# Norms at the borders between stages: squares summed as the rows come, roots on 128x4, the first two tiles of the next product by row block, the output in pieces

## The chip, the cores and the metric

One NeuronCore of a Trainium2 chip. The metric is the device time of one execution in microseconds. Five engines matter: PE (TensorE, matmuls), DVE (VectorE), ACT (ScalarE), POOL (GpSimd) and SP (SyncE, which only issues transfers here). Each runs its own list of instructions in order and waits on semaphores.

## What is computed

Two transformer blocks over one sequence of 512 tokens and 1024 channels, all in float32. The first block has sliding-window attention and a gated linear attention, then a product-key expert layer ("peer"); the second has a feed-forward, latent attention with a gated delta rule, and another feed-forward. What matters here is the normalization in front of the products, seven times in all:

```python
def rmsnorm(x, g):
    xf = x.astype(jnp.float32)
    xf = xf * lax.rsqrt(jnp.mean(xf * xf, axis=-1, keepdims=True) + EPS)
    return (xf * g.astype(jnp.float32)).astype(x.dtype)

def modulate(x, g, shift, scale):
    return rmsnorm(x, g) * (1.0 + scale[:, None, :]) + shift[:, None, :]

h = modulate(x, g_ffn1[l], sh1, sc1)
x = x + 0.5 * gt1[:, None, :] * swiglu(h, w1_gate[l], w1_up[l], w1_down[l])
h = modulate(x, g_mix[l], sh2, sc2)
proj = h @ w_in[l]
...
h = modulate(x, g_ffn2[l], sh3, sc3)
x = x + 0.5 * gt3[:, None, :] * swiglu(h, w2_gate[l], w2_up[l], w2_down[l])
return rmsnorm(x, g_final)
```

## The kernel before, in words

X lies in on-chip memory transposed: 128 channels on the partitions, eight row blocks of 512 tokens side by side (`X[:, k, :]`). The program is a list of stages (L2442 to L2479), and each engine runs its part of each stage in that order: ada1, swa, gla, wout1, query, gates, dense, fin, norm1, ffn1, mix2, delta, state, b1, latent, heads, b2, wout2, ffn2, end. `behind(e, tag)` (L129) makes an engine wait until all four engines have ended a stage. `Marks` (L41) is a semaphore with named values: `then_inc(instruction, key)` counts up after an instruction, `wait_ge(engine, key)` waits for it.

**Weights.** SP loads tiles of 512 KB into a ring of four raw slots (`w_load`, L189). Tiles of kind "split" are turned into two parts: `w_hi` (L207) rounds on ACT, `w_lo` (L216) takes the rest on DVE, into two slots, so the high part of tile i waits until PE has ended tile i-2. `pe_three` (L222) multiplies a tile: for each of eight row blocks three matmuls of 512 columns (high x high, high x low, low x high), 24 in all. `pe_plain` (L233) is the plain float32 product; each float32 matmul shows as two records in the trace.

**A norm** (L293 to L341). ACT squares the eight blocks into four buffers, PE multiplies each square with a 128x128 matrix of ones and adds all eight in bank 0, so that every partition has the sum of each token; DVE takes mean plus epsilon (L308), ACT the root (L299), DVE the reciprocal (L310), all over 128x512. `Modulated` (L313) then has DVE multiply each block by its weight (L330, ahead) and by the reciprocal (L336), ACT add the shift and round it to the high part (L322), and DVE take the low part (L339). PE waits for all eight low parts (L957, L1410, L1583) before the first tile. The final norms scale X itself (L1379, L2437).

The norms are: n1 in ada1 (L414 to L450), n2 ahead of query (L954 to L1002), nf in norm1 and f1 at the head of ffn1, one behind the other (L1367 to L1380, L1406), m2 in mix2 (L1580), f2 at the head of ffn2, ne in end (L2425). In each the work begins behind the previous stage.

**Stages around them.** wout1 (L843) and wout2 (L2394) are eight tiles each, with a residual (L354) by DVE behind each; wout1 has three groups of column sums for the second block's conditioning (`Ada2`, L262) between its tiles. A feed-forward (L1384) multiplies 44 tiles (gate and up in turn), writes high and low parts of 22 hidden blocks, and then 24 down tiles, three for each output block. Its loop over tiles on ACT and DVE splits tile t+1 in iteration t, ahead of the work on tile t:

```python
            for t in range(2 * FF):
                w_lo(e, self.all[t + 1])
```

PE waits for the last hidden block (L1417) between up and down. In query, 16 tiles are followed each by four small matmuls (L970), whose scores DVE copies (L1000) and sorts (`top16`). mix2 first multiplies two narrow tiles (8 columns, t_ab), then a chain on ACT and DVE (L1601 to L1644) with small transposes on PE (L1591), then the qkv tiles. `Branch` (L2067) is b1 and b2; behind b2, the sum YG is split block by block (L346, L351) before wout2. At the end SP waits for all engines and stores X in one transfer (L2505 to L2508).

## Time and profile before

| | |
|---|---|
| time, median of 3 runs | 4030.22 us (4027.99 to 4030.34) |
| the profiled execution, its own time | 4036.27 us |
| its span, first to last instruction | 4034.5 us |
| mean granted TensorE clock | 0.902 |
| PE busy | 3478.3 us, 86% |
| DVE busy | 2137.5 us, 53% |
| ACT busy | 1478.1 us, 37% |
| POOL busy | 740.4 us, 18% |

The profile is one execution as the hardware profiler saw it. Times are in microseconds unless marked ns. "L304" is a line of the kernel. In a timeline a row has the start, the duration from the first to the last of the merged instructions, engine, line, operation, output <- inputs with the shape, the count, and in brackets how long the engine was idle before it and who released it. PEclk is the granted TensorE clock as a share of 2.4 GHz: 1.00, or 0.50 for 1.2 GHz.

### The profile page before, as it was taken

The numbers are of one execution on the slowest core, as the hardware profiler recorded it, in microseconds if no ns is written. First come the engines' busy times: TensorE is split into PE (matmuls) and PEld (weight loads), VectorE is DVE, ScalarE is ACT, GpSimd is POOL, SyncE is SP. The second block draws the span as 40 slices with busy tenths as digits, with TensorE's granted clock in tenths as the row PEclk, the third lists the DMA queues.
The fourth block names the chain that finished last, engine by engine and source line by source line (L and its number), as shares of the span: only waits on it lengthen the run. The fifth ranks groups of instructions, "written<-read, shape, count | busy, mean of one in ns | idle before, by whom it ended". The sixth has DMA issues, their size and how long they took to land.

```text
span 4034.5 us, 40391 instructions
## 1 busy us (share of the span) xinstructions
PE 3478.3 (86%) x16091; PEld 2792.1 (69%) x16091; DVE 2137.5 (53%) x3519; ACT 1478.1 (37%) x2397; POOL 740.4 (18%) x597
## 2 busy tenths in 40 slices
PE   5887883669999999999699977787897898788998
PEld 2466473569999999999488856576666754567886
DVE  2445699967666666666555335565323213334332
ACT  1221115965555555555322224343212212223221
POOL 0100105855444444444100000000000000000000
PEclk7886996889999999999799988898888996899999
DMA  4420511367777777777155321110001120222221
GB/s 165 139 96 16 177 48 45 136 236 292 279 278 279 279 277 276 278 277 256 58 188 187 119 82 47 37 42 1 22 21 63 58 63 0 97 70 84 99 93 69
DMA packets 169292, 537.41 MB, mean 133 GB/s; under 512 B 13840, under 2 KB 65424, under 8 KB 150672
## 3 DMA queue, kind: packets, MB, share of 16 engines
q1 hardware_dynamic: 135696, 346.06, 24.3%
q0 software_dynamic: 33408, 188.76, 12.6%
q8 instruction: 128, 2.10, 0.2%
q14 instruction: 60, 0.49, 0.0%
HBM read 505.41 MB, written 29.36 MB: 133 GB/s over the span
## 4 chain that ended last, share of the span: by engine, by line
PE 77%; DVE 17%; ACT 3%; DMA 2%; issue 1%; SPq 0%; DVEq 0%; ACTq 0%
PE ps L228 10%; PE ps L229 10%; PE ps L230 10%; PE ps L237 5%; PE ps L1277 4%; PE ps L1278 4%; PE ps L1263 4%; PE ps L1261 4%; PE ps L1262 4%; PE ps L1276 4%; DVE peerg_OH L1100 2%; PE ps L304 1%; PE ps L168 1%; PE ps L459 1%; PE ps L255 1%
## 5 line engine op out<-in xcount | busy, mean ns | idle before, releaser
L220 DVE TENSOR_TENSOR Wl<-W,Wh 128x1024 fp32r<-128x1024 f32 x363 | 437.4, 1207 | 581.8 <-ACT Wh L214 581.5
L214 ACT ACTIVATE Wh<-W 128x1024 fp32r<-128x1024 f32 x363 | 375.4, 1036 | 308.3 <-PE ps L230 270.0
L1240 POOL TENSOR_TENSOR peer_Y<-peer_Y,peerv_UV 128x1024 f32<-128x1024 f32 x128 | 379.8, 2967 | 533.7 <-ACT peerv_UV L1301 533.7
L1261 PE MATMUL ps<-peer_Hh,Wh 128*128 128x384 f32 x1024 | 344.4, 336 | 8.4 <-DVE Wl L220 8.4
L1263 PE MATMUL ps<-peer_Hh,Wl 128*128 128x384 f32 x1024 | 344.4, 336 | 0.0
L1262 PE MATMUL ps<-peer_Hl,Wh 128*128 128x384 f32 x1024 | 343.7, 336 | 0.0
L228 PE MATMUL ps<-f_Hh,Wh 128*128 128x512 f32 x704 | 276.9, 393 | 34.2 <-DVE Wl L220 34.2
L1278 PE MATMUL ps<-peerv_VH,peerv_HTl 128*128 128x512 f32 x768 | 301.3, 392 | 0.0
L1277 PE MATMUL ps<-peerv_VL,peerv_HTh 128*128 128x512 f32 x768 | 301.0, 392 | 0.0
L1276 PE MATMUL ps<-peerv_VH,peerv_HTh 128*128 128x512 f32 x768 | 298.7, 389 | 0.9 <-DVE peerv_HTl L1333 0.9
L229 PE MATMUL ps<-f_Hl,Wh 128*128 128x512 f32 x704 | 275.8, 392 | 0.0
L230 PE MATMUL ps<-f_Hh,Wl 128*128 128x512 f32 x704 | 275.7, 392 | 0.0
L1330 DVE TENSOR_TENSOR peerv_TG<-peerv_TG,peerv_GR 128x384 f32<-128x384 f32 x128 | 197.3, 1542 | 141.5 <-ACT peerv_TG L1306 141.5
L228 PE MATMUL ps<-mix_Hh,Wh 128*128 128x512 f32 (+1 forms) x472 | 201.8, 427 | 65.0 <-DVE Wl L220 43.2
L1261 PEld LDWEIGHTS ps<-peer_Hh,Wh 128*128 128x128 f32 x1024 | 192.9, 188 | 13.8 <-DVE Wl L220 8.9
L1262 PEld LDWEIGHTS ps<-peer_Hl,Wh 128*128 128x128 f32 x1024 | 192.8, 188 | 4.9
L1165 PE MATMUL ps<-peerg_OH 128*128 128x128 f32 x768 | 128.7, 333 | 78.1 <-DVE peerg_OH L1100 53.7
L229 PE MATMUL ps<-mix_Hl,Wh 128*128 128x512 f32 (+1 forms) x472 | 195.8, 415 | 0.0
L230 PE MATMUL ps<-mix_Hh,Wl 128*128 128x512 f32 (+1 forms) x472 | 194.2, 412 | 0.0
L1263 PEld LDWEIGHTS ps<-peer_Hh,Wl 128*128 128x128 f32 x1024 | 192.7, 188 | 0.0
L1199 DVE TENSOR_TENSOR peerv_VL<-peerv_VR,peerv_VH 128x1024 fp32r<-128x1024 f32 x128 | 156.8, 1225 | 61.9 <-ACT peerv_VH L1195 61.9
L1165 PEld LDWEIGHTS ps<-peerg_OH 128*128 128x128 f32 x768 | 117.3, 239 | 89.9 <-DVE peerg_OH L1100 69.0
(483 smaller groups left out, 6966.0 us busy)
## 6 DMA issues: line engine op xcount, KB each, us to landing
W<-peer_u SPq DMA_DIRECT2D x128, 512.0 KB, 7.2
peerv_VR<-peer_v SPq DMA_DIRECT2D x128, 512.0 KB, 3.4
gates_dram<-peerg_GB SPq DMA_DIRECT2D x12, 2048.0 KB, 6.8
peerv_GR<-gates_dram SPq DMA_DIRECT2D x32, 768.0 KB, 7.9
f_AW<-w_ada POOLq DMA_DIRECT2D x48, 512.0 KB, 4.3
W<-w_gate SPq DMA_DIRECT2D x44, 512.0 KB, 4.0
W<-w_up SPq DMA_DIRECT2D x44, 512.0 KB, 3.2
swa_AW<-w_ada POOLq DMA_DIRECT2D x32, 512.0 KB, 5.0
```

What stands on the lines that cost most here:

```text
L214: A.then_inc(e.activation(w_parts(i)[0], w_raw(i), ACT.Copy), ("w_hi", i))
L220: V.then_inc(e.tensor_tensor(lo, w_raw(i), hi.bitcast(F32), SUB), ("w", i))
L228: e.matmul(o[0:m, :], hi[:, j, :], rhs[0][:, k, :], start=k == 0, stop=False)
L229: e.matmul(o[0:m, :], hi[:, j, :], rhs[1][:, k, :], start=False, stop=False)
L230: ins = e.matmul(o[0:m, :], lo[:, j, :], rhs[0][:, k, :], start=False, stop=k == nk - 1)
L1240: G.then_inc(e.tensor_tensor(Y, Y, UV[:, k % NUV, 1024:2048], ADD), ("y", k))
L1261: e.matmul(o, hi[:, k, :], H2[0][:, k, 0:TD], start=k == 0, stop=False)
L1262: e.matmul(o, hi[:, k, :], H2[1][:, k, 0:TD], start=False, stop=False)
L1263: ins = e.matmul(o, lo[:, k, :], H2[0][:, k, 0:TD], start=False, stop=k == 7)
L1276: e.matmul(o, HTh[:, s, sl], VH[:, s, d], start=n == 0, stop=False)
L1277: e.matmul(o, HTh[:, s, sl], VL[:, s, d], start=False, stop=False)
L1278: ins = e.matmul(o, HTl[:, s, sl], VH[:, s, d], start=False, stop=n == 127)
```

## The change

- `Norm` replaces the three `rstd` functions. The sum of a block is four matmuls of one column: the squares are the weights, a column of ones the moving operand, so that tokens come to lie on the partitions, one bank column for each block. DVE adds the eight columns (128x4), mean, root and reciprocal run on 128x4, DVE spreads the result on a diagonal (128x512), and one matmul with ones broadcasts it. DVE multiplies X by weight and broadcast in one instruction from the bank (`scale_dve`). Squares lie in three buffers.
- n2, m2, f2 and ne: squares and sums are taken in the stage before, a block's sum behind the tile two blocks later; the last two behind the stage's last tile. nf's follow the residuals of fin, f1's follow the scaling of X by nf. The stage norm1 is gone.
- The first two tiles of the next product are split in the stage before, and `pe_two` multiplies both by row block, as low parts come. The loops in query and in the feed-forward then split tile t+2 in iteration t.
- mix2 splits its first qkv tile ahead of the chain; b2 splits the blocks of YG in its loop; the output goes in eight transfers.

```diff
+    class Norm:
+        def __init__(self, tag, bank, ready):
+            self.tag, self.bank, self.ready, self.s = tag, ps(bank), ready, tiny(4)
+
+        def square(self, k):
+            return DG_t[:, 512 * (k % 3):512 * (k % 3) + 512]
+
+        def sq_act(self, e, k):
+            self.ready(e, k)
+            if k >= 3:
+                PE.wait_ge(e, (self.tag, "sq", k - 3))
+            A.then_inc(e.activation(self.square(k), X[:, k, :], ACT.Square), (self.tag, "sq", k))
+
+        def sq_pe(self, e, k):
+            A.wait_ge(e, (self.tag, "sq", k))
+            for tb, sl in enumerate(sl4):
+                ins = e.matmul(self.bank[:, 8 * tb + k:8 * tb + k + 1], self.square(k)[:, sl], ones[:, 0:1],
+                               start=True, stop=True)
+            PE.then_inc(ins, (self.tag, "sq", k))
+
+        def mean_dve(self, e):
+            PE.wait_ge(e, (self.tag, "sq", 7))
+            V.then_inc(e.tensor_reduce(self.s, self.bank[:, 0:32].rearrange("p (b k) -> p b k", b=4), AX.X, ADD))
+            V.wait_ge(e, V.n)
+            V.then_inc(e.tensor_scalar(self.s, self.s, 1.0 / D, EPS, MUL, ADD), (self.tag, "mean"))
+
+        def root_act(self, e):
+            V.wait_ge(e, (self.tag, "mean"))
+            A.then_inc(e.activation(self.s, self.s, ACT.Sqrt), (self.tag, "root"))
+
+        def root_dve(self, e):
+            A.wait_ge(e, (self.tag, "root"))
+            V.then_inc(e.reciprocal(self.s, self.s))
+            V.wait_ge(e, V.n)
+            V.then_inc(e.tensor_tensor(v4(self.square(8)), bc4(ident), self.s.unsqueeze(2).broadcast_to([128, 4, 128]),
+                                       MUL), (self.tag, "diag"))
+
+        def root_pe(self, e):
+            V.wait_ge(e, (self.tag, "diag"))
+            PE.then_inc(e.matmul(self.bank, ones, self.square(8), start=True, stop=True), (self.tag, "rstd"))
+
+        def scale_dve(self, e, k, o, w, *keys):
+
+            PE.wait_ge(e, (self.tag, "rstd"))
+            V.then_inc(e.scalar_tensor_tensor(out=o, in0=X[:, k, :], scalar=w[:, k:k + 1], in1=self.bank, op0=MUL,
+                                              op1=MUL), *keys)
...
+            self.norm.mean_dve(e)
+            self.norm.root_dve(e)
+            behind(e, self.before)
             for k in range(9):
                 if k < 8:
-                    V.wait_ge(e, (self.tag, "rstd"))
-                    x = self.xw[:, k, :]
-                    V.then_inc(e.tensor_tensor(x, x, self.r, MUL), (self.tag, "xr", k))
+                    if k >= 3:
+                        V.wait_ge(e, (self.tag, "lo", k - 3))
+                    self.norm.scale_dve(e, k, self.xr[:, k % 3, :], self.w, (self.tag, "xr", k))
                 if k:
                     A.wait_ge(e, (self.tag, "hi", k - 1))
                     V.then_inc(e.scalar_tensor_tensor(
-                        out=self.lo[:, k - 1, :], in0=self.xw[:, k - 1, :], scalar=self.shift[:, k - 1:k],
+                        out=self.lo[:, k - 1, :], in0=self.xr[:, (k - 1) % 3, :], scalar=self.shift[:, k - 1:k],
                         in1=self.hi[:, k - 1, :].bitcast(F32), op0=ADD, op1=SUB), (self.tag, "lo", k - 1))
...
+        def pe_two(self, e, outs, ts, m, keys):
+
+            w = [[x.rearrange("p (k m) -> p k m", k=8) for x in w_parts(i)] for i in ts]
+            steps = [(t, k) for k in range(6) for t in (0, 1)] + [(t, k) for t in (0, 1) for k in (6, 7)]
+            for i in ts:
+                V.wait_ge(e, ("w", i))
+            for t, k in steps:
+                V.wait_ge(e, (self.tag, "lo", k))
+                o, (hi, lo) = outs[t][0:m, :], w[t]
+                e.matmul(o, hi[:, k, :], self.hi[:, k, :], start=k == 0, stop=False)
+                e.matmul(o, hi[:, k, :], self.lo[:, k, :], start=False, stop=False)
+                ins = e.matmul(o, lo[:, k, :], self.hi[:, k, :], start=False, stop=k == 7)
+                if k == 7:
+                    PE.then_inc(ins, ("w", ts[t]), keys[t])
...
+            if nb >= 2:
+                n2n.sq_pe(e, nb - 2)
         ada2a.pe(e, 2)
+        n2n.sq_pe(e, 6)
+        n2n.sq_pe(e, 7)
...
+            if nb == 7:
+                w_lo(e, t_q[0])
             if nb == 5:
                 ada2a.dve(e, 0)
             for n in range(3 * nb, 3 * nb + 3):
...
+                   "w2")
+
+    def wout1_act(e):
+        for k in range(8):
+            n2n.sq_act(e, k)
+            if k in (5, 6):
+                w_hi(e, t_q[k - 5])
 
...
+        n2.norm.root_pe(e)
+        n2.pe_two(e, [ps(1), ps(2)], t_q[0:2], 128, [("q", 0), ("q", 1)])
+        for nb in range(1, 17):
+            if 2 <= nb < 16:
+                A.wait_ge(e, ("qt", nb - 2))
+                pe_three(e, ps(1 + nb % 2), t_q[nb], 8, 128, H2, 0, 8, ("q", nb))
...
-                w_hi(e, t_q[nb + 1])
+            if nb < 14:
+                w_hi(e, t_q[nb + 2])
             PE.wait_ge(e, ("q", nb))
             if nb >= 2:
                 PE.wait_ge(e, ("sub", nb - 2))
-            A.then_inc(e.activation(QT[:, nb % 2, :], ps(nb % 2), ACT.Copy), ("qt", nb))
...
         for nb in range(17):
-            if nb < 15:
-                w_lo(e, t_q[nb + 1])
+            if nb < 14:
+                w_lo(e, t_q[nb + 2])
...
             A.then_inc(e.activation(YB[:, blk, 0:512], ps(2 + 2 * blk), ACT.Copy), ("yb", blk))
+        for k in range(8):
+            nf.sq_act(e, k)
+        nf.root_act(e)
+        for k in range(8):
+            f1n.sq_act(e, k)
+            if k < 2:
+                w_hi(e, ff1.all[k])
 
     def fin_dve(e):
...
             residual(e, k, mod1[:, 40:48], ps(FIN_BANK[k]), ("x2", k))
+        ff1.scales(e)
+        nf.mean_dve(e)
+        nf.root_dve(e)
+        for k in range(8):
+            nf.scale_dve(e, k, X[:, k, :], vec("final_norm_w"), ("x3", k))
+        for i in ff1.all[0:2]:
+            w_lo(e, i)
...
+                if nb >= 2:
+                    then.sq_pe(e, nb - 2)
+            then.sq_pe(e, 6)
+            then.sq_pe(e, 7)
...
             self.norm.act(e)
-            w_hi(e, self.all[0])
             for t in range(2 * FF):
-                w_hi(e, self.all[t + 1])
+                w_hi(e, self.all[t + 2])
                 nb = t // 2
...
-            for i in self.all[2 * FF + 1:]:
+            for n, i in enumerate((self.all + ahead)[2 * FF + 2:]):
                 w_hi(e, i)
-
-        def dve(self, e):
+                if n % 3 == 1 and n >= 4:
+                    then.sq_act(e, n // 3 - 1)
+            for k in range(7 if ahead else 6, 8):
+                then.sq_act(e, k)
+
+        def dve(self, e, ahead):
             tag = self.tag
-            behind(e, self.before)
-            V.then_inc(e.scalar_tensor_tensor(out=self.wc, in0=mod2[:, self.m0 + 8:self.m0 + 16], scalar=1.0,
-                                              in1=vec(self.g), op0=ADD, op1=MUL), (tag, "wc"))
-            V.then_inc(e.tensor_scalar(self.hg, mod2[:, self.m0 + 16:self.m0 + 24], 0.5, None, MUL))
-            V.wait_ge(e, V.n)
+            V.wait_ge(e, (tag, "hg"))
             self.norm.dve(e)
-            w_lo(e, self.all[0])
             for t in range(2 * FF):
-                w_lo(e, self.all[t + 1])
+                w_lo(e, self.all[t + 2])
...
                 w_lo(e, i)
                 if self.ada:
                     self.ada.mac(e, 2 * FF + n)
                     if n == 9:
                         self.ada.dve(e, 5)
-                if n >= 3 and n % 3 == 0:
-                    self.x(e, n // 3 - 1)
-            self.x(e, 7)
+                if n % 3 == 2:
+                    self.x(e, n // 3)
+            for nb in range(len(rest) // 3, 8):
+                self.x(e, nb)
 
         def x(self, e, nb):
             PE.wait_ge(e, (self.tag, "d", nb))
             residual(e, nb, self.hg, ps(5 + nb % 3), (self.tag, "x", nb))
 
-    ff1 = FeedForward("f1", "w1", "g_ffn1_2", 0, "norm1", (3, 6))
+    ff1 = FeedForward(f1n, "w1", "g_ffn1_2", 0, "fin", (3, 6))
...
     def mix2_sp(e):
+        for i in t_ab + t_qkv[0:1]:
+            w_load(e, i)
         behind(e, "ffn1")
...
     def mix2_pe(e):
-        behind(e, "ffn1")
-        n4.pe(e)
-        V.wait_ge(e, ("m2", "lo", 7))
-        for s in range(2):
-            pe_three(e, ps(1 + s), t_ab[s], 8, 8, H4, 0, 8, ("ab", s))
+        m2n.root_pe(e)
+        n4.pe_two(e, [ps(2), ps(3)], t_ab, 8, [("ab", 0), ("ab", 1)])
...
         n4.act(e)
-        for i in t_ab:
-            w_hi(e, i)
+        w_hi(e, t_qkv[0])
         PE.wait_ge(e, ("ab", 1))
-        A.then_inc(e.activation(bb[0:8, :], ps(2)[0:8, :], ACT.Sigmoid), "bb")
+        A.then_inc(e.activation(bb[0:8, :], ps(3)[0:8, :], ACT.Sigmoid), "bb")
...
         n4.dve(e)
-        for i in t_ab:
-            w_lo(e, i)
+        w_lo(e, t_qkv[0])
         PE.wait_ge(e, ("ab", 0))
-        V.then_inc(e.tensor_copy(ab[0:8, :], ps(1)[0:8, :]), "ab0")
+        V.then_inc(e.tensor_copy(ab[0:8, :], ps(2)[0:8, :]), "ab0")
...
-                    if self.add:
+                    if self.sums:
                         V.then_inc(e.tensor_tensor(g, g, ps(4 + t % 4), MUL), (tag, "out", t))
                         V.wait_ge(e, (tag, "out", t))
                         V.then_inc(e.tensor_tensor(y, y, g, ADD), (tag, "y", nb))
+                        if nb:
+                            self.sum_dve(e, nb - 1)
...
+        for n, i in enumerate(t_wo2 + ff2.all[0:2]):
             w_hi(e, i)
+            if n >= 4:
+                f2n.sq_act(e, n - 4)
+        for k in range(6, 8):
+            f2n.sq_act(e, k)
...
+        ff2.scales(e)
         x_back.wait_ge(e, "x")
-        for nb in range(9):
-            if nb < 8:
-                w_lo(e, t_wo2[nb])
-            if nb:
-                PE.wait_ge(e, ("wout2", nb - 1))
...
+        for n, i in enumerate(t_wo2 + ff2.all[0:2]):
+            w_lo(e, i)
+            if n >= 2:
+                PE.wait_ge(e, ("wout2", n - 2))
+                residual(e, n - 2, mod2[:, 40:48], ps((n - 2) % 4), ("x4", n - 2))
...
         if "query" in on:
+            for i in t_q[:3]:
+                w_load(e, i)
             query_sp(e)
-            for i in t_q:
+            for i in t_q[3:]:
...
-        for m in engines:
-            m.wait_ge(e, m.last)
-        out_done.then_inc(e.dma_start(out.rearrange("(k p) t -> p k t", p=128), X), "out")
+        for k in range(8):
+            if upto == "end":
+                V.wait_ge(e, ("out", k))
+            else:
+                behind(e, upto)
+            out_done.then_inc(e.dma_start(out[k * 128:k * 128 + 128, :], X[:, k, :]), "out")
         out_done.wait_ge(e, "out")
```

## Rows read from the trace of the kernel before

**Rows 1.** Busy times in windows, the five borders (window, its length, engines' busy time and counts, granted clock, DMA share, GB/s).
```profile
455.70:482.70 27.00, 8.81 (x33) 4.58 (x31) 20.01 (x31) 12.80 (x19) 0.00 (x0) 0.78 0.30 117
1937.50:1994.10 56.60, 23.51 (x65) 11.44 (x65) 35.97 (x51) 21.54 (x33) 2.35 (x3) 0.69 0.08 28
2371.30:2395.80 24.50, 7.11 (x17) 2.96 (x16) 18.84 (x30) 13.19 (x21) 0.00 (x0) 0.72 0.15 46
3617.90:3643.70 25.80, 7.11 (x16) 2.97 (x17) 20.04 (x31) 14.51 (x21) 0.00 (x0) 0.76 0.00 0
4007.80:4034.50 26.70, 7.13 (x16) 2.96 (x16) 10.16 (x11) 6.51 (x10) 0.00 (x0) 0.74 0.22 79
```

**Rows 2.** Timeline from wout1 to query, then two windows of its first tiles.
```profile
458.56 7.10 PE L304 MATMUL ps<-peerq_SQ,consts_sb 128*128 128x512 f32 x16 [1.15 <-ACT peerq_SQ L297]
...
470.48 1.29 DVE L336 TENSOR_TENSOR peerq_XW<-peerq_XW,peerq_RS 128x512 f32<-128x512 f32 x2
...
471.96 0.75 DVE L339 SCALAR_TENSOR_TENSOR peer_Hl<-peerq_XW,small,peer_Hh 128x512 fp32r<-128x512 f32 x1 [0.19 <-ACT peer_Hh L322]
...
482.74 0.76 PE L228 MATMUL ps<-peer_Hh,Wh 128*128 128x512 f32 x1 [17.08 <-DVE Wl L220]
...
482.80:487.40 4.60, 4.60 (x11) 3.63 (x12) 0.93 (x1) 0.00 (x0) 0.00 (x0) 0.50 0.70 219
488.00:494.00 6.00, 6.00 (x28) 4.95 (x27) 1.23 (x1) 1.55 (x2) 0.00 (x0) 1.00 0.00 0
```

**Rows 3.** Timeline of TensorE, one-column sums in three stages, and a window.
```profile
40.90 3.57 PE L255 MATMUL ps<-consts_sb,ada_ACC 128*128 128x1 f32 x16 [16.27 <-DVE ada_ACC L251]
...
446.91 1.84 PE L255 MATMUL ps<-consts_sb,adaw_AA 128*128 128x1 f32 x16
448.62 7.11 PE L237 MATMUL ps<-mix_MX,W 128*128 128x512 f32 x16
...
3224.26 6.22 PE L2141 MATMUL ps<-consts_sb,X 128*128 128x1 f32 x48
...
3229.00:3235.00 6.00, 6.00 (x13) 3.42 (x14) 0.35 (x2) 0.04 (x1) 0.00 (x0) 0.50 0.01 3
```

**Rows 4.** Timeline of the delta stage: scalar step, diagonal and broadcast of a norm.
```profile
2701.61 1.02 PE L1684 MATMUL ps<-DG,consts_sb 128*128 128x512 f32 x2
...
2718.51 0.16 DVE L1733 TENSOR_SCALAR small<-ps 128x4 f32<-128x4 f32 x1 [7.33 <-PE ps L1692]
...
2719.16 0.69 DVE L1737 TENSOR_TENSOR DG<-consts_sb,small 128x512 f32<-128x512 f32 x1
```

**Rows 5.** Timeline of the first stage and of fin and norm1, and a window.
```profile
14.96 9.67 PE L304 MATMUL ps<-ada_SQ,consts_sb 128*128 128x512 f32 x16 [14.96 <-ACT ada_SQ L297]
...
30.19 6.84 DVE L251 SCALAR_TENSOR_TENSOR ada_ACC<-W,small,ada_ACC 128x1024 f32<-128x1024 f32 x5
...
1942.72 0.27 PE L168 MATMUL ps<-consts_sb,peer_Y 128*128 128x128 f32 x1
...
1945.00:1946.00 1.00, 0.00 (x0) 0.00 (x0) 0.33 (x1) 0.58 (x2) 0.00 (x0) 0.62 0.00 0
...
1961.10 5.39 DVE L1379 SCALAR_TENSOR_TENSOR X<-X,vecs_sb,norm_RS 128x512 f32<-128x512 f32 x8
```

**Rows 6.** TensorE's waits in ffn1 (in total, times, longest), and its timeline there.
```profile
PE ps L228 <- DVE f_HFl L1472: 2.2, 1, 2.2
...
2246.98 1.04 ACT L214 ACTIVATE Wh<-W 128x1024 fp32r<-128x1024 f32 x1
...
2248.05 1.23 DVE L220 TENSOR_TENSOR Wl<-W,Wh 128x1024 fp32r<-128x1024 f32 x1 [0.26 <-ACT Wh L214]
```

**Rows 7.** Timeline of TensorE at the end of mix2.
```profile
2423.27 0.76 PE L228 MATMUL ps<-mix_Hh,Wh 128*128 128x512 f32 x1 [3.09 <-DVE Wl L220]
```

**Rows 8.** Timeline of TensorE at the start of wout2.
```profile
3571.70 0.77 PE L228 MATMUL ps<-mlao_Yh,Wh 128*128 128x512 f32 x1 [8.33 <-DVE Wl L220]
```

**Rows 9.** DMA issues by line: size of each, median us to landing.
```profile
W<-w_down SPq DMA_DIRECT2D x16, 384.0 KB, 2.9
```

More of the change, by code:

```diff
@@ L290, in dve @@
             across_dve(e, self.bank, "b_ada_2", self.g0 + i, mod2, (self.tag, "across", i), ("mod2", self.g0 + i))
-    def rstd_act(e, tag, sq, r):
-        for k in range(8):
-            if k >= 4:
-                PE.wait_ge(e, (tag, "sq", k - 4))
-            A.then_inc(e.activation(sq[:, k % 4, :], X[:, k, :], ACT.Square), (tag, "sq", k))
-        V.wait_ge(e, (tag, "mean"))
-        A.then_inc(e.activation(r, r, ACT.Sqrt), (tag, "root"))
-    def rstd_pe(e, tag, sq):
-        for k in range(8):
-            A.wait_ge(e, (tag, "sq", k))
-            PE.then_inc(e.matmul(ps(0), ones, sq[:, k % 4, :], start=k == 0, stop=k == 7), (tag, "sq", k))
@@ L386, in build @@
     PG = Phase("adaw")
[L387 removed]
+    ada2a = Ada2("ada2a", 0, 3, PG, 1, 2)
     PG.end()
@@ L918, in build @@
     P3.end()
-    P3 = Phase("norm")
-    rsf, sqf = P3.t("RS", 512), P3.t("SQ", 2048, k=4)
-    P3.end()
     PP.end()
@@ L1363, in fin_pe, with __init__ @@
             PE.then_inc(ins, ("yt", k))
-    def norm1_act(e):
-        behind(e, "fin")
-        rstd_act(e, "nf", sqf, rsf)
-    def norm1_pe(e):
-        rstd_pe(e, "nf", sqf)
-    def norm1_dve(e):
-        behind(e, "fin")
-        rstd_dve(e, "nf", rsf)
-        V.wait_ge(e, ("nf", "rstd"))
         for k in range(8):
-            V.then_inc(e.scalar_tensor_tensor(out=X[:, k, :], in0=X[:, k, :], scalar=vec("final_norm_w")[:, k:k + 1],
-                                              in1=rsf, op0=MUL, op1=MUL), ("x3", k))
+            nf.sq_pe(e, k)
+        nf.root_pe(e)
+        for k in range(8):
+            f1n.sq_pe(e, k)
     class FeedForward:
-        def __init__(self, tag, n, g, m0, before, ada=None):
-            self.tag, self.g, self.m0, self.before = tag, g, m0, before
+        def __init__(self, norm, n, g, m0, before, ada=None):
+            self.tag = tag = norm.tag
+            self.g, self.m0, self.before = g, m0, before
             P = Phase(tag)
@@ L1473, in dve @@
                                (tag, "hf", nb))
-            rest = self.all[2 * FF + 1:]
+            rest = (self.all + ahead)[2 * FF + 2:]
             for n, i in enumerate(rest):
@@ L2517, in build @@
     for program in (tensor, vector, scalar, gpsimd, sync):
-        for m in engines:
-            m.last = m.n
         program(Tally())
```

194 lines of the change are left out of this document (90 added, 104 removed).

## The prediction

> **What bounds the kernel.** I read the busy times of the stretches between products first. At five borders TensorE is nearly empty: from the last matmul of one product to the first of the next pass 27.0, 56.6, 24.5 and 25.8 us, and 26.7 us from the last one to the end [rows 1], 160.6 us of 4034.5. Elsewhere, in the products, its matmuls stand back to back, so a stretch of it that becomes longer or shorter moves the end. The timeline of the first border shows what fills it: eight full-width sums on PE (7.10 us, to 465.66), mean, root and reciprocal over 512 columns, products and low parts of all eight row blocks (from 470.48), the split of the first weight tile, and only then a matmul at 482.74, 17.08 us after PE's last [rows 2]. Nothing there runs beside anything useful. The borders end one another in turn, so what one gives reaches the end, unless the product behind it meets a later wait.
>
> I count from the profiled execution, 4036.27 us. The median of the runs, 4030.22, is 6.05 lower; the gain is taken over unchanged. About 0.2% (8 us) is what a measurement can tell here.
>
> **Costs common to the borders.** (a) A new sum of a block is four matmuls of one column. Two such sums (16 records) take 1.71 us from their start to the next matmul when PE is hot, so 0.85 each (446.91 to 448.62); in the cold clock 3.57 for two, 1.78 each (at 40.90) [rows 3]. A dense product now holds five of them ahead of its end: +4.25 us; the old eight cost 7.10, but in the gap. (b) From the last sum to the diagonal: a reduce (0.2, like its neighbours) and then what the other norms of this kernel do in 1.34 us (2718.51 to 2719.85); the broadcast matmul takes 1.02 and its weights 0.25 [rows 4]. Together 2.9 with small waits; a cold broadcast adds 0.3. Before, from the last sum to the first product took 4.8 (465.66 to 470.48) [rows 2]. (c) PE starts when block 0 has its low part, 2.2 us after the first product begins (470.48 to 472.71), not after all eight and a weight split [rows 2]. DVE needs 1.3 us per further block; the six matmuls per block of two tiles need 2.6 cold (0.43 each: 11 in 4.6 us) and 1.4 hot (0.23 each: 26 in 6 us, besides two at the window's edges) [rows 2], so DVE keeps ahead, and two tiles last as long as before: some 12 of 48 cold, 13.3 us.
>
> **The clock.** At 3224.26 PE issued 48 one-column records back to back. It was never idle, yet from 3229 the granted clock stands at 0.50, 1.2 GHz, until past 3235, by when full-width matmuls had long followed [rows 3]. So I price sums that follow one another outside a product at the cold value once the clock has fallen. The Trainium skill says otherwise in words (TensorE: Matmul & The Clock Gate, Part 1 and its table of goals): activity releases the throttle, keep TensorE busy and it stays warm. By that rule the sums would get hot by themselves, a rival below; this trace does not agree.
>
> **The edits, border by border.**
> *First norm (n1).* PE is cold there; 8 x 1.78 = 14.2 us from 14.96 give 29.2, then 1.6 to the diagonal and 0.75 for a first multiply: the first multiply-add at 31.6, before at 30.19 [rows 5]. The rest of that stage hangs on DVE and the ring of four weight slots, and moves by **+1.4**. Bounds: -3 (hot after some 5 us, as the old sums there) to +2.
> *Query.* Last tile ends 4.25 later; then a sum, the last ada column sums (1.7) and two sums: 4.25, then 2.9 + 2.2 + 0.35 for one cold sum and latency: first matmul 13.95 after the old end, before 27.0. Gain 13.05. The weight split of tile 2 waits for tile 0, which now ends only six matmuls ahead of tile 1, and DVE splits tile 3 ahead of its first copy of scores: copy 1.5 later after tile 1, but one split (1.1) leaves the DVE chain behind it, which sets that stage: -0.4. **12.6.** SP issues three peer_wq tiles earlier and waits with the subkeys as before; these land long before tile 1 ends.
> *fin, f1.* PE's transposes end at 1943; the sums follow hot for some 2.6 us (the clock fell between 1945 and 1946 before), then cold [rows 5]: 3 x 0.87 + 5 x 1.78 = 11.5, end 1954.7. Cold chain 3.3, so the scaling of X starts at 1958.1, before 1961.10 [rows 5]. The f1 sums run cold, one behind each scaled block: from 1959.5, 14.3 us, to 1973.8; chain 3.3, low part 2.2: first matmul 1979.4, before 1994.1. Gain 14.7. Splits of the first tiles are ready by then.
> *Weight splits two tiles ahead, ffn1 and ffn2.* The third tile waits for its split, which waits for the first tile: 1.05 + 1.23 + latency less the 1.36 of six matmuls = -1.1. And the step from up to down, which looks untouched, gets a new wait. Before, PE waited 2.2 us there for product, high and low part of the last block [rows 6]. Now ACT and DVE do the split of tile all[45] first, and it can start only when PE has ended tile 43: 1.04 + 1.23 us ahead of that chain [rows 6], and in ffn1 a multiply-add (1.37, as each of the five at 30.19) behind it on DVE. -3.7 in ffn1, -2.25 in ffn2. The gap grows to 5.9 and 4.5; more cold matmuls after it: -1.0 and -1.3 (bounds 0 to 2.7 each). f1: 14.7 - 1.1 - 3.7 - 1.0 = **8.9.**
> *m2.* 4.25; two sums, then block 7, whose residual now stands behind the small splits of t_ab (+0.6), square 0.65, sum: last sum at +3.0, chain 2.9, low 2.2, latency 0.2: 12.55 against 24.5, gain 11.95. Abs now waits behind split, copy and add: -1.6. The first qkv tile is split early: the wait of 3.09 after the small transposes goes [rows 7], +3.1. **13.4.**
> *y.* Eight blocks and a tile are split while PE idles 8.33 us, from 3563.4 [rows 8]. Now block 7 only: product, add, high and low part (0.7 each), two small scales (0.35), one tile's low part (1.23, with its high part beside the block's): first matmul 3567.9 instead of 3571.70. **3.8.**
> *f2.* 4.25; the residual of block 7 stands behind split 9, which waits for the last tile: +3.15, square, sum at 4.8, one cold sum 0.3, chain 2.9, low 2.2: 14.55 against 25.8. 11.25 - 1.1 - 2.25 - 1.3 = **6.6.**
> *End.* 4.25; last sum +2.65 (block 7's residual 0.78, square, sum), chain 2.9 with the Sqrt table, eight scalings 5.4 (as 1961.10) [rows 5], one last piece of 256 KB instead of 2 MB: 384 KB land in 2.9 us [rows 9], I take 2.9 for it, and 0.5 of SP and waits. 18.7 against 26.7: **8.0.** Bounds 6 to 9 (queueing behind seven pieces that come every 0.67 us; 2 us for the piece).
> The squares on ACT, the banks and the buffers cost nothing: each square stands between splits that are due later; without that cover a square is 0.65.
>
> Sum: 12.6 + 8.9 + 13.4 + 3.8 + 6.6 + 8.0 - 1.4 = 51.9. 4036.3 - 51.9 = 3984.4; as a median **3978**. Bounds of its own: dense sums 0.78 to 0.95 (20 of them, -2 to +2), clock and gaps +-5, pieces +-2: 3969 to 3989.
>
> **Rivals.**
> A. *The one-column sums run hot.* For: full-width matmuls get hot after some 5 us. Against: 3224 to 3230 [rows 3]. f1: sums of fin end 1950, scaling 1952.9, f1's first matmul 1966.4 instead of 1979.4; first norm 4.7 less: 17.7 more gain, 3961. By the Trainium skill's rule above this is the time. Chance 0.10.
> B. *The pass by row block stays cold* because PE waits in it, four times 48 matmuls at 0.427 = 20.5 instead of 13.3: +28, 4007, still faster. For: at each start the clock is cold. Against: 2.6 us of matmuls per block stand against 1.3 of DVE, so there is no wait. Part of it (one or two borders) lies in 3985 to 3993. Chance 0.08.
> C. *Slower.* The sums inside the products let the clock fall, since such matmuls don't keep it up. Price: a restart costs 12 matmuls x 0.2 = 2.4 plus a cold sum's 0.9, 3.3 each, 20 times 66: 4044. It decides from 2.6 us each (51.9 / 20), and is slower by over 0.2% from 3.0. Against: sixteen such records at 446.91 in a dense stretch, and the 16 records behind took 7.11 us, 0.44 each, the same as the full-width sums of 7.10 [rows 2, 3]. Chance 0.02.
> D. *The new waits are longer than priced* (another queue wait inside the products): half of the gain, 4004. Chance 0.05.
> Forecast as above: 0.75.
>
> **How the numbers follow.** Likeliest 3978. The range takes the forecast's own and A at its lower end, and the first part of B and D at the upper: 3961 to 3992, leaving out some 0.2. Faster by over 0.2%: forecast, A, B, D, 0.96 (all but a little of D); within it 0.02; slower 0.02.
>
> **What would show it.** In the changed profile: five gaps of about 10 to 14 us with one-column sums in them; clock 0.50 during the f1 sums with PE busy; first matmul of a product some 2 us behind the first product on DVE, before the eighth; the wait for HFl between up and down grown from 2.2 to about 6 in ffn1 and 4.5 in ffn2; no idle 3.09 ahead of the first qkv tile; output issues as eight rows, the last within 0.1 us of the last scaling. Wrong would be: sums at 0.87 throughout (A), a matmul step of 0.43 through all 48 (B), cold clock inside ffn down stages (C), or unpredicted waits on split tiles (D).

## The result, and the profile after

The changed kernel takes 4042.27 us (median of 9 runs, 4041.22 to 4044.57), the kernel before 4030.22 (median of 9, 4021.02 to 4033.75): a ratio of 1.0034, interval 1.0024 to 1.0045. It is slower by 12 us, where 3978 was forecast, 52 faster. The profiled execution of it took 4041.22 us, span 4039.4.

I laid the two traces side by side at the first and last matmul of each product (in us; the last column is what the stretch gained or lost, the one before it what the prediction said).

| stretch | before | after | said | measured |
|---|---|---|---|---|
| first norm, to wout1's first matmul | 396.96 | 396.67 | +1.4 | -0.3 |
| wout1, first to last matmul | 58.8 | 64.9 | +4.25 | +6.2 |
| wout1 to query's first matmul | 27.0 | 10.6 | -17.3 | -16.4 |
| query's first matmul to dense's last | 1454.8 | 1455.3 | +0.4 | +0.5 |
| dense to ffn1's first matmul | 56.6 | 39.6 | -14.7 | -17.0 |
| **ffn1, gate and up tiles** | 251.6 | 290.5 | +1.1 | **+38.9** |
| up to down, ffn1 | 2.2 | 5.8 | +3.7 | +3.7 |
| ffn1, down tiles | 123.4 | 129.2 | +5.25 | +5.7 |
| ffn1 to mix2's first matmul | 24.5 | 9.5 | -16.2 | -15.0 |
| mix2's first matmul to b2's last | 1167.5 | 1164.0 | -1.5 | -3.5 |
| b2 to wout2's first matmul | 8.3 | 4.5 | -3.8 | -3.8 |
| **wout2, first to last matmul** | 46.2 | 67.4 | +4.25 | **+21.2** |
| wout2 to ffn2's first matmul | 25.8 | 12.2 | -15.5 | -13.6 |
| ffn2, gate and up tiles | 241.9 | 243.2 | +1.1 | +1.3 |
| up to down, ffn2 | 2.2 | 4.5 | +2.25 | +2.3 |
| ffn2, down tiles | 120.0 | 127.6 | +5.55 | +7.6 |
| last matmul of ffn2 to the end | 26.7 | 13.9 | -12.25 | -12.8 |

The columns add up to 51.9 us less, as said (52.0 by the rounded rows), and 5.0 more, as measured. The five borders behaved, to within 2.3 us each. What ate the gain lies inside two products that the prediction took to be back to back: 37.8 us in ffn1's gate and up tiles and 17.0 in wout2, 54.8 together.

The five borders of the changed kernel, as busy times in windows (window, its length, busy time and count of PE, its weight loads, DVE, ACT, POOL, then granted clock, DMA share, GB/s). They answer to [rows 1]:

```profile
464.20:472.20 8.00, 3.84 (x18) 2.19 (x18) 4.78 (x11) 1.54 (x3) 0.00 (x0) 0.66 0.62 236
1927.60:1967.20 39.60, 30.50 (x165) 27.24 (x165) 19.82 (x35) 16.24 (x26) 1.67 (x3) 0.63 0.20 66
2392.70:2402.20 9.50, 5.00 (x26) 3.25 (x26) 4.42 (x11) 3.71 (x6) 0.00 (x0) 0.64 0.18 55
3638.20:3650.30 12.10, 6.17 (x26) 4.52 (x27) 5.39 (x10) 5.55 (x8) 0.00 (x0) 0.62 0.13 43
4025.60:4039.40 13.80, 4.08 (x25) 2.73 (x24) 7.31 (x13) 2.12 (x3) 0.00 (x0) 0.67 0.40 152
```

The windows before added up to 160.6 us, these add up to 83.0.

Then PE's waits in the whole changed kernel (in total, times, longest). Of the rows shown, the last is new. In the first, 15.0 us are the wait for the program's first square, which the kernel before has too, and 10.4 are new and lie at wout2:

```profile
PE ps L310 <- ACT DG L305: 27.1, 9, 15.0
...
PE ps L255 <- DVE f_AA L251: 19.3, 5, 3.9
```

L255 are the column sums of the conditioning (`Ada2`), which ffn1 carries along between its tiles. Neither the diff nor my prediction speaks of them as touched. The three engines around the first of them, in timelines of the changed kernel:

```profile
2014.30 0.39 PE L230 MATMUL ps<-f_Hh,Wl 128*128 128x512 f32 x1
2018.54 2.39 PE L255 MATMUL ps<-consts_sb,f_AA 128*128 128x1 f32 x16 [3.85 <-DVE f_AA L251]
2020.79 0.77 PE L228 MATMUL ps<-f_Hh,Wh 128*128 128x512 f32 x1
```

```profile
2014.78 1.06 ACT L214 ACTIVATE Wh<-W 128x1024 fp32r<-128x1024 f32 x1 [3.90 <-PE ps L230]
```

```profile
2015.87 1.23 DVE L220 TENSOR_TENSOR Wl<-W,Wh 128x1024 fp32r<-128x1024 f32 x1 [2.82 <-ACT Wh L214]
2017.20 1.28 DVE L251 SCALAR_TENSOR_TENSOR f_AA<-f_AW,small,f_AA 128x1024 f32<-128x1024 f32 x1
```

PE ends tile 7 at 2014.7 and wants the sums of accumulator 0. The last multiply-add into it stands in DVE's iteration 7, behind the split of tile 9. That split needs a slot that tile 7 holds. So the split starts only when PE has ended tile 7: 1.06 on ACT, 1.23 and 1.28 on DVE, and PE waits 3.85 us for all three. Before, iteration 7 split tile 8, into the slot of tile 6, and its multiply-add was done at 2039.75, 0.7 us before PE came for the sums at 2040.45 (1.05 us before at the other four). The cover was thin. DVE's timeline of the kernel before:

```profile
2036.79 1.23 DVE L220 TENSOR_TENSOR Wl<-W,Wh 128x1024 fp32r<-128x1024 f32 x1 [2.06 <-ACT Wh L214]
2038.47 1.28 DVE L251 SCALAR_TENSOR_TENSOR f_AA<-f_AW,small,f_AA 128x1024 f32<-128x1024 f32 x1 [0.46 <-DVE Wl L220]
```

In the changed kernel the wait comes five times, and each time the clock falls. The windows are the wait, the stretch behind it, and the tiles up to the next wait:

```profile
2014.70:2019.00 4.30, 0.46 (x4) 0.46 (x5) 3.03 (x3) 1.06 (x1) 0.22 (x1) 1.00 0.53 179
2019.90:2026.70 6.80, 6.80 (x20) 5.54 (x20) 0.57 (x1) 0.00 (x0) 0.00 (x0) 0.50 0.22 80
2026.70:2067.00 40.30, 40.30 (x179) 33.30 (x178) 20.90 (x21) 11.26 (x14) 3.70 (x7) 1.00 0.49 170
```

Five waits are 19.25 us. The rest of the 37.8, 18.5 or 3.7 for each wait, is PE at half speed behind them.

In wout2 it is the same shape with ACT in the middle. Its queue in the changed kernel, and PE's sum:

```profile
3590.03 1.06 ACT L214 ACTIVATE Wh<-W 128x1024 fp32r<-128x1024 f32 x1 [4.38 <-PE ps L230]
3591.00 0.61 ACT L305 ACTIVATE DG<-X 128x512 f32<-128x512 f32 x1
```

```profile
3589.55 0.39 PE L230 MATMUL ps<-mlao_Yh,Wl 128*128 128x512 f32 x1
3591.66 1.05 PE L310 MATMUL ps<-consts_sb,DG 128*128 128x1 f32 x8 [1.73 <-ACT DG L305]
3592.58 0.48 PE L228 MATMUL ps<-mlao_Yh,Wh 128*128 128x512 f32 x1
```

ACT takes the square of block n-4 behind the high part of tile n. The high part waits until PE has ended tile n-2, and right behind that tile PE wants the sum of block n-4. The waits from 3565 to 3640 (PE's, in total, times, longest) are six of 1.73, five inside wout2 and one behind it:

```profile
PE ps L310 <- ACT DG L305: 10.4, 6, 1.7
```

Inside wout2 the five waits are 8.7 of the 17.0 us; the rest is again mostly PE at half speed, behind four of the five.

### The profile page after: what moved, and what is told of

It is laid out like the page before. It is cut to its first block, busy times and chain, and to the rows that moved or that the text cites. A ratio compares the mean times of both kernels' runs of the same rounds, so it can differ in the third digit from the quotient of the medians.

```text
span 4039.4 us, 41152 instructions
## 1 busy us (share of the span) xinstructions
PE 3534.0 (87%) x16441; PEld 2863.0 (71%) x16441; DVE 2102.5 (52%) x3501; ACT 1479.5 (37%) x2397; POOL 738.3 (18%) x597
## 4 chain that ended last, share of the span: by engine, by line
PE 78%; DVE 16%; ACT 3%; DMA 2%; issue 1%; SPq 0%; DVEq 0%; ACTq 0%
PE ps L228 10%; PE ps L229 10%; PE ps L230 10%; PE ps L237 5%; PE ps L1327 4%; PE ps L1328 4%; PE ps L1313 4%; PE ps L1311 4%; PE ps L1312 4%; PE ps L1326 4%; DVE peerg_OH L1150 2%; PE ps L310 2%; PE ps L255 1%; PE ps L168 1%; DVE Wl L220 1%; PE ps L507 1%
## 5 line engine op out<-in xcount | busy, mean ns | idle before, releaser
L228 PE MATMUL ps<-f_Hh,Wh 128*128 128x512 f32 x672 | 266.9, 397 | 2.2 <-DVE Wl L220 2.2
L229 PE MATMUL ps<-f_Hl,Wh 128*128 128x512 f32 x672 | 265.4, 395 | 0.0
L230 PE MATMUL ps<-f_Hh,Wl 128*128 128x512 f32 x672 | 265.1, 395 | 0.0
L228 PE MATMUL ps<-mix_Hh,Wh 128*128 128x512 f32 x456 | 194.3, 426 | 45.7 <-DVE Wl L220 23.4
L229 PE MATMUL ps<-mix_Hl,Wh 128*128 128x512 f32 x456 | 188.5, 413 | 0.0
L230 PE MATMUL ps<-mix_Hh,Wl 128*128 128x512 f32 x456 | 187.4, 411 | 0.0
```

What stands on the lines that cost most here:

```text
L228: e.matmul(o[0:m, :], hi[:, j, :], rhs[0][:, k, :], start=k == 0, stop=False)
L229: e.matmul(o[0:m, :], hi[:, j, :], rhs[1][:, k, :], start=False, stop=False)
L230: ins = e.matmul(o[0:m, :], lo[:, j, :], rhs[0][:, k, :], start=False, stop=k == nk - 1)
```

## The experiments

All kernels are compared with the kernel before in the same job, whose medians were 4030.2, 4027.1, 4030.0 and 4032.7; experiments that have the changed kernel as base stand against its 4042.3. **Theory W**: work that waits for PE's tile was put ahead of work that PE waits for behind the same tile; the cost is the wait and the half-speed stretch behind it. **Rival S**: the one-column sums themselves let the clock fall. **Rival M**: weight transfers are late. "Hot" and "cold" stand for a granted clock of 1.00 and 0.50; a one-column record is one of the two that a one-column float32 matmul leaves in the trace, so a block's sum is eight of them.

**e1, the multiply-add ahead of the split** (ffn1, DVE):

```diff
             for t in range(2 * FF):
-                w_lo(e, self.all[t + 2])
                 if self.ada:
-                    if t % 8 == 1 and t > 8:
-                        self.ada.dve(e, t // 8 - 1)
                     self.ada.mac(e, t)
+                w_lo(e, self.all[t + 2])
+                if self.ada and t % 8 == 1 and t > 8:
+                    self.ada.dve(e, t // 8 - 1)
```

> Edit: in ffn1 DVE does the multiply-add of the conditioning of iteration t ahead of the split of tile t+2, not behind it. Theory W (a wait with its price in clock): the five waits of 3.85 us ahead of the column sums vanish, and so do the 13 or so matmuls at half speed behind each (38.9 us that ffn1's gate and up tiles grew by, less 5 x 3.85 = 19.3, is 19.6): 4042 becomes 4003. Rival S (the one-column sums themselves let the clock fall, wait or not): only the 19.3 go, 4023, and the granted clock still falls behind the sums. Rival M (the 38.9 us come from weight transfers that are late): 4042, no change.

Measured: 4003.51 us (4000.64 to 4005.06), ratio to before 0.9937, 0.9920 to 0.9953. Gate and up tiles take 252.8 us instead of 290.5. A window from the third tile to the last, of e1:

```profile
1982.70:2220.60 237.90, 237.90 (x1088) 198.01 (x1088) 131.12 (x132) 68.38 (x85) 22.72 (x43) 1.00 0.58 187
```

PE is never idle in it, and the clock is 1.00 throughout, with all five groups of sixteen one-column records inside. S and M fall for this stage. Moving two lines is worth 38.8 us, and the one edit alone puts the changed kernel ahead of the one before. (The step from up to down also fell by 1.4, to 4.45: the multiply-add of 1.28 no longer stands in that chain, which the expectation had left out.)

**e2, the square ahead of the high part** (wout2, ACT):

```diff
-            w_hi(e, i)
             if n >= 4:
                 f2n.sq_act(e, n - 4)
+            w_hi(e, i)
```

> Edit: in wout2 ACT takes the square of block n-4 ahead of the high part of tile n, not behind it. The high part waits until PE has ended tile n-2, and PE's sum of block n-4 stands right behind that tile. Theory W: the five waits of 1.9 us inside wout2 vanish with the slow matmuls behind them, and wout2 shrinks by 21.2 - 4.25 = 17.0 us: 4025. Rival S: the waits go, 5 x 1.9 = 9.4, and the clock still falls behind the sums: 4033.

Measured: 4024.36 us (4019.80 to 4028.50), ratio 0.9993, 0.9984 to 1.0003. wout2 takes 51.2 us instead of 67.4; what is left of these waits is, in PE's waits of e2 from 3570 to 3634:

```profile
PE ps L310 <- ACT DG L305: 1.6, 2, 0.9
```

The five sums between tiles stand back to back with the matmuls, clock 1.00; the 1.6 us lie behind the last tile. 51.2 is 5.0 above the kernel before, for five sums priced at 4.25.

**e3, both, and the second down tile's split behind the last hidden block:**

```diff
 @@ ACT, in the loop over tiles @@
-                w_hi(e, self.all[t + 2])
+                if t < 2 * FF - 1:
+                    w_hi(e, self.all[t + 2])
 @@ ACT, behind the loop @@
+            w_hi(e, self.all[2 * FF + 1])
 @@ DVE, in the loop over tiles @@
-                w_lo(e, self.all[t + 2])
+                if t < 2 * FF - 1:
+                    w_lo(e, self.all[t + 2])
 @@ DVE, behind the loop @@
+            w_lo(e, self.all[2 * FF + 1])
```

> Edit: both of the above, and ACT and DVE split the second down tile behind the last hidden block instead of ahead of it, in both feed-forwards. Theory W: 38.9 + 17.0, and the step from up to down goes back from 5.8 and 4.45 to 2.2 us each (5.9), with some 1 us of slow matmuls behind: 4042 - 62 = 3980, what the prediction said for the change, plus 2. Rival S: 19.3 + 9.4 + 6: 4007.

Measured: 3978.00 us (3975.51 to 3982.81), ratio 0.9880, 0.9863 to 0.9896. PE's waits of e3 from 1980 to 2349, in ffn1 and behind it:

```profile
PE ps L228 <- DVE f_HFl L1542: 2.2, 1, 2.2
PE ps L310 <- ACT DG L305: 0.3, 1, 0.3
```

The step from up to down is back at 2.2, as in [rows 6], and so is ffn2's. The change with three orders of work put right gives 49 us against the before of its job. No run has the third edit alone; e1 and e2 together give 56.7 of e3's 64.3, which leaves 7.6 for it, where 6.9 was expected.

**e4, the wait without the sums behind it** (ffn1, PE):

```diff
                 if self.ada and t % 8 == 7:
-                    self.ada.pe(e, t // 8)
+                    V.wait_ge(e, (self.ada.tag, "mac", t))
+                if self.ada and t % 8 == 0 and t:
+                    self.ada.pe(e, t // 8 - 1)
```

> Edit: in ffn1 PE still waits for the multiply-adds behind tiles 7, 15, 23, 31, 39, but issues the sixteen one-column records of their sums one tile later, so that full matmuls follow the wait at once. If the wait alone lets the clock fall: 4042 as the changed kernel, clock 0.50 behind each wait. If it takes the wait and the one-column matmuls together: the 19.6 us of slow matmuls go and the waits stay, 4022.

Measured: 4031.84 us (4027.15 to 4034.59), between the two. PE's waits of e4 in ffn1, and windows of one wait, of the slow stretch behind it and of the tiles that follow:

```profile
PE ps L228 <- DVE f_AA L251: 19.3, 5, 3.9
```

```profile
2010.60:2014.60 4.00, 0.15 (x1) 0.00 (x0) 2.56 (x3) 1.06 (x1) 0.00 (x0) 1.00 0.47 160
2016.10:2019.40 3.30, 3.30 (x9) 2.55 (x8) 0.44 (x1) 0.00 (x0) 0.00 (x0) 0.50 0.47 158
2019.50:2061.00 41.50, 41.50 (x192) 34.60 (x191) 20.91 (x21) 11.25 (x14) 3.59 (x7) 1.00 0.49 160
```

The waits are what they were, 3.85 each, and the clock still falls behind every one, but behind this one it is cold for 3.3 us of the window instead of 6.8. Gate and up tiles take 282.3: against e1's 252.8, less the waits, that is 2.0 us of slow matmuls for each wait; with the sums straight behind the wait it was 3.7. So the wait alone lets the clock fall, and sixteen one-column records behind it nearly double what that costs. Neither branch of the expectation was right alone. The Trainium skill (TensorE: Matmul & The Clock Gate, "HAM oscillation — how this bites in real kernels") tells of a kernel whose loop waits for a transfer each time round and pays for a fall of the clock each time; the five waits here agree.

**e5, no row-block pass.** Base of e5 to e8: e3, 3978.0.

```diff
-            for i in ts:
-                V.wait_ge(e, ("w", i))
-            for t, k in steps:
...
+            V.wait_ge(e, (self.tag, "lo", 7))
+            for t in (0, 1):
+                pe_three(e, outs[t], ts[t], 8, m, (self.hi, self.lo), 0, 8, keys[t])
```

> Base: the kernel with the three edits (3978.0). Edit: the first two tiles of query, ffn1, mix2 and ffn2 wait for the low part of all eight blocks and are then multiplied one after the other, as every other tile. From the first to the eighth low part DVE takes 8.8 us at each of the four borders; the wait of 1.1 us ahead of the third tile goes at three of them. By the prediction's reading (PE is never held up within the row-block pass): 4 x 8.8 - 3 x 1.1 = 32 more: 4010. If the row-block pass stayed cold for its length (rival B of the prediction), the two orders would cost the same to within some 5 us: 3978 to 3985.

Measured: 4009.95 us (4006.83 to 4016.59), ratio 0.9949, 0.9933 to 0.9966. PE's waits of e5 ahead of the first tiles of ffn1 and mix2 (in the row-block pass of the changed kernel they are 2.6 and 2.5 us):

```profile
PE ps L228 <- DVE f_Hl L366: 11.4, 1, 11.4
PE ps L228 <- DVE mix_Hl L366: 11.3, 1, 11.3
```

The row-block pass is worth 32 us of the change's gain at the borders. Rival B of the prediction falls; the pass is cold for its first 9 to 12 matmuls, as every product's start, and hot for the rest: from the first to the last of its 48 starts it takes 12.4 to 13.1 us in the changed kernel, said 13.3.

**e6, the output in one transfer:**

```diff
-        for k in range(8):
...
-            out_done.then_inc(e.dma_start(out[k * 128:k * 128 + 128, :], X[:, k, :]), "out")
+        V.wait_ge(e, ("out", 7))
+        out_done.then_inc(e.dma_start(out.rearrange("(k p) t -> p k t", p=128), X), "out")
```

> Base: the kernel with the three edits. Edit: the output leaves in one transfer of 2 MB behind the last scaling. The transfer takes 7.3 us as in the kernel before instead of 2.2 for the last piece: 5 more, 3983. If the pieces queued behind one another, the gain would be smaller and the whole within 2 us: 3980.

Measured: 3976.05 us (two runs, 3974.53 and 3977.57), lower than either number expected, which by itself would say that the pieces bring nothing. The profile says where to look. DMA issues of e3, then of e6 (KB each, us from issue to landing):

```profile
out<-X SPq DMA_DIRECT2D x8, 256.0 KB, 2.2
```

```profile
out<-X SPq DMA_DIRECT2D x1, 2048.0 KB, 7.2
```

From ffn2's last matmul to the end of the span, e3 has 3973.7 - 3959.6 = 14.1 us and e6 19.3 (to 3975.8), so the pieces are worth 5.2 at that place. e6's stream merely came there 3.2 us earlier, through stretches in which the two kernels do not differ. Ahead of wout1 the changed kernel and e1 to e9 do not differ, yet its first matmul lies between 391.9 and 396.8 in them: a difference of a few us between single profiles, or between medians of two runs, is not to be read without its place.

**e7, squares and sums behind the last tile** (mix2's, ffn2's and the last norm; PE's part, ACT's squares are moved alike):

```diff
-                if nb >= 2:
-                    then.sq_pe(e, nb - 2)
-            then.sq_pe(e, 6)
-            then.sq_pe(e, 7)
+            for k in range(8):
+                then.sq_pe(e, k)
```

> Base: the kernel with the three edits. Edit: for the norms of mix2, ffn2 and end, ACT's squares and PE's sums stand behind the last tile of the stage ahead, all eight, not between its tiles (the one-column form stays). Cold theory, as the prediction priced it: three sums at 0.85 and five at 1.78 us = 11.5 from the last tile to the last sum, against 3.5, 5.65 and 2.6 now, and 4.05 less inside each stage: 10.5 more, 3988. Hot rival (one-column sums keep the clock up): 6.8 per border, 3.5 less in all: 3974.

Measured: 3988.36 us (3986.51 to 3990.21), ratio 0.9897, 0.9880 to 0.9913. The sums behind wout2 in e7, and two windows of them:

```profile
3580.34 12.17 PE L310 MATMUL ps<-consts_sb,DG 128*128 128x1 f32 x64 [1.73 <-ACT DG L305]
```

```profile
3578.50:3582.00 3.50, 1.77 (x16) 1.67 (x15) 1.89 (x2) 3.13 (x5) 0.00 (x0) 1.00 0.00 0
3582.30:3592.10 9.80, 9.80 (x47) 9.80 (x48) 0.00 (x0) 3.80 (x5) 0.00 (x0) 0.50 0.11 46
```

64 one-column records, back to back behind a wait of 1.73: the clock falls 1.8 us after their start and stays down while PE is busy for 9.8. The changed kernel's own trace says the same: of the two norms behind dense, the first one's eight sums begin in a hot stretch, and the second one's are cold from end to end (clock 0.50 from 1938 to 1972), 13.81 us where 14.3 was said:

```profile
1932.84 8.99 PE L310 MATMUL ps<-consts_sb,DG 128*128 128x1 f32 x64
1947.07 13.81 PE L310 MATMUL ps<-consts_sb,DG 128*128 128x1 f32 x64 [1.50 <-ACT DG L305]
```

The cold reading of [rows 3] holds; rival A of the prediction falls, and with it, for matmuls of this form, the rule that it drew on (Trainium skill, TensorE: Matmul & The Clock Gate, Part 1). Squares and sums between the tiles of the stage ahead are worth 10 us at three borders.

**e8, a version that goes further**, three more places where PE waits for what it does not yet need:

```diff
 @@ PE, from up to down: wait for the hidden blocks that the tile reads @@
-            V.wait_ge(e, (tag, "hf", FF - 1))
                 for i, k0, n in self.down[nb]:
+                    if nb == 0:
+                        V.wait_ge(e, (tag, "hf", k0 + n - 1))
 @@ row-block pass: four blocks of both tiles, then the rest of each @@
-            steps = [(t, k) for k in range(6) for t in (0, 1)] + [(t, k) for t in (0, 1) for k in (6, 7)]
+            steps = [(t, k) for k in range(4) for t in (0, 1)] + [(t, k) for t in (0, 1) for k in range(4, 8)]
 @@ mix2, PE: the first qkv tile ahead of the wait for the scalar chain @@
         n4.pe_two(e, [ps(2), ps(3)], t_ab, 8, [("ab", 0), ("ab", 1)])
+        pe_three(e, ps(0), t_qkv[0], 8, 128, H4, 0, 8, ("qkv", 0))
 @@ delta, PE: the first qkv tile goes from its old place @@
-                pe_three(e, ps(n % 2), t_qkv[n], 8, 128, H4, 0, 8, ("qkv", n))
+                if n:
+                    pe_three(e, ps(n % 2), t_qkv[n], 8, 128, H4, 0, 8, ("qkv", n))
```

> Base: the kernel with the three edits. Edits: (1) PE waits for the last hidden block ahead of the third down tile, which is the first that reads it, not ahead of the first: 2 x 2.17 us and the slow matmuls behind (1.0 and 2.4): 7.7 less. (2) The row-block pass takes both tiles for blocks 0 to 3 and then the rest of tile 0 and of tile 1, so that the third tile's split is done when the pass ends: 2 x 1.1 + 0.33 = 2.5 less. (3) PE multiplies the first qkv tile in the 11.75 us in which it waits for the scalar chain of mix2: 5.4 less, or nothing, if DVE and ACT set the delta stage behind it. Together 3962, or 3968 if (3) brings nothing.

Measured: 3964.18 us (3961.56 to 3965.85), ratio 0.9840, 0.9823 to 0.9856: the fastest here, 1.6% below the kernel before. PE's waits of e8 from 1980 to 2349 are only these two:

```profile
PE ps L333 <- DVE DG L328: 1.7, 1, 1.7
PE ps L310 <- ACT DG L305: 0.3, 1, 0.3
```

Edits 1 and 2 do what was expected in kind: both steps from up to down are gone, no wait of 1.1 for a third tile is left in the same view from 1958 on or in ffn2, and ffn2's down tiles take 124.6 instead of 126.3. Over both feed-forwards that is 9.0 of the 10.2 expected. What the early qkv tile brings is less sure. The first column sum behind it starts 35.2 us after mix2's first matmul, against 39.2 to 41.5 in the changed kernel and e1 to e7, so it brings about 4 us there. From mix2's first matmul to b1's, e8 takes 761.1 and e3 766.6, which looks like the 5.4; but e6, which has the tile in its old place, takes 761.1 too, and e7 769.1. So these two traces do not show that its gain reaches the end. No run has edit 3 alone.

**e9, one sum moved** (wout1, base e8):

```diff
+            if nb == 7:
+                n2n.sq_pe(e, 4)
-            if nb >= 2:
+            if nb >= 2 and nb != 6:
                 n2n.sq_pe(e, nb - 2)
```

> Base: the kernel of e8 (3964.2). Edit: in wout1 the norm's sum of block 4 moves from behind tile 6, where it stands with the sixteen records of the conditioning's sums (24 one-column records in a row, 2.6 us, and then the clock at 0.50 and tile 7 in 8.65 us instead of 6.95), to behind tile 7. If a long enough row of one-column records lets the clock fall without any wait: between tiles 6 and 7 stand sixteen, the clock stays at 1.00 there, and tile 7 takes 6.95: 1.7 less from wout1's first matmul to its last, which only the profile can tell. If the fall at that place has another cause, tile 7 stays at 8.65.

Measured: 3964.29 us (3963.73 and 3964.85). TensorE's timeline of e9 around the tile in question:

```profile
449.05 1.84 PE L255 MATMUL ps<-consts_sb,adaw_AA 128*128 128x1 f32 x16
450.75 7.11 PE L237 MATMUL ps<-mix_MX,W 128*128 128x512 f32 x16
457.70 1.84 PE L310 MATMUL ps<-consts_sb,DG 128*128 128x1 f32 x16
```

The tile takes 7.11, or 6.95 from its start to the next one's, but this alone shows little: in e8, its base, that tile was hot too and the one behind the other group of 24 slow. Over all traces it is plainer. wout1 has two such groups of 24 in each of the changed kernel and e1 to e8, and one in e9: 19 groups, and 10 of them are followed by a tile that is 1.7 us slower. Behind the three groups of sixteen between wout1's tiles (two in the kernel before, one in e9) there was no such tile. So a row of 24 can let the clock fall without any wait, and none of the three rows of 16 did, nor the five in ffn1 of e1. It is not an even chance at either place: behind tile 6 it came in 8 of 9 traces, behind tile 3 in 2 of 10. Why, stays open.

## Why the prediction was wrong

**The step that failed** is the one on weight splits two tiles ahead. It found the rule: a split moved two tiles ahead starts only when PE has ended the tile before, and whatever stands behind it on ACT and DVE is late for a PE that wants it at once. It found one place, the step from up to down, and priced it well (said +3.7 and +2.25, measured +3.7 and +2.3). It did not ask the same question at each of PE's other waits in that loop. The column sums behind tiles 7, 15, 23, 31 and 39 are such a wait, five times, with 3.6 us ahead of them in queues (1.06, 1.23, and 1.28 for the multiply-add, which the text had at 1.37), each price already there. That was 37.8 us (e1: 38.8 in the total).

**The second failure** is one sentence: the squares on ACT "cost nothing: each square stands between splits that are due later". In the feed-forwards this is so, three tiles to a block. In wout2, one tile to a block, the split ahead of the square is released by the very tile behind which PE wants the sum: 17.0 us (e2: 17.9 in the total). The sentence named the cover but did not look at what releases it.

**Point by point**, the smaller terms:

- Sums inside a dense stage, said 0.85: 0.81 from start to start where nothing waits (e3), 1.0 with what they disturb in wout2.
- First norm, said +1.4: its first multiply-add was at 31.23 (said 31.6, before 30.19), and by wout1 nothing of it can be told.
- Query: the gap was 10.6, said 9.7.
- f1: the sums of the first norm there stayed hot longer (8.99 us for eight, said 11.5), 2.3 better.
- mix2 and f2: 1.2 and 1.9 worse; 0.9 of each is the chain from the last sum to the first scaling, 3.84 us where 2.9 was said, since its broadcast ran cold (2.07 for its two records, the 1.02 of [rows 4] with 0.3 added for a cold one was too little), and the rest are last sums that go partly cold.
- The first qkv tile: 0.6 nearer to mix2's first matmul than before, said 1.5, since 0.78 of the wait of 3.09 stays; the stretch behind it varies by several us between traces (e8).
- Output: 0.6 better, pieces of 2.2 us.
- Down tiles of ffn2: 2.0 worse, 1.5 of it slow matmuls behind the wait of 4.5.
- wout1: 1.9 worse, 1.7 of it behind 24 one-column records in a row.

All rows of the table but those of the two steps above differ from what was said by 2.1 us together; the two steps are 54.8 of the 56.9 by which the traces differ from the sum (4036.27 - 4041.22 = -5.0 instead of 51.9). By the medians it is 64; the before's profiled execution was 6.05 above its median and this one 1.05 below, and no stage can be named for these 7.

**The rivals.** D, another queue wait inside the products, was right in kind and far too small: I gave it half of the gain and 0.05. C put its price right in form, a fall of the clock and a cold sum, 3.3 us, and found that it would have to come at twenty places; it came at ten, and at 5.5 us each (54.8 / 10), since there was a wait in front; the clock fell behind nine of them. I treated waits and clock as two rivals with small chances. They are one: where the clock falls behind it, a wait of a few us in a hot product costs itself and half as much again or more. A and B fell (e7, e5); by its own sum A was 3960, not 3961. The bounds I gave held for most terms, and were missed by little at two: the sums in wout2 took 1.0 each (bound 0.95, e2), the slow matmuls behind ffn2's step from up to down 2.8 us (bound 2.7). The range was too narrow because it had no term for a wait that I had not looked for.

**Order of the borders.** e3 shows that the reading of the borders was sound: with the two orders put right, and the third that the prediction had priced as a loss, the change takes 3978.0. That this is the very number of the forecast is luck. Without the loss of the third order (3.7 + 2.25 + 1.0 + 1.3 = 8.25) the prediction's own terms give 3970. By the two profiled executions e3 is 60.8 us faster than the kernel before (4036.27 - 3975.51), and the terms give 51.9 + 8.25 = 60.2; by the medians it is 49 to 52.

## What to carry to other kernels

When work is moved further ahead in an in-order queue, write down for the moved instruction what releases it now. Then go through every wait of the engine that does the releasing, and ask for each whether what it waits for stands behind the moved instruction: in a ring of two slots, "two tiles ahead" means "not before PE ends this tile", and PE must want nothing from that queue at this tile's end. If it does, put the short piece that PE waits for first (e1 and e2: a few lines, 39 and 18 us).
